# The second feed-forward matmul of a hybrid decoder block as seven block products, with weight sums made by DMA

## What is computed

```python
D_MODEL = 1024; SEQ = 512; D_FF = 4 * D_MODEL
...
        h = rms_norm(x, g_ffn_norm[l])
        x = x + jnp.square(jax.nn.relu(h @ w_ff1[l])) @ w_ff2[l]
```

## Time and profile before

| | |
|---|---|
| median of 3 runs | 634.78 us (633.72 to 634.92) |
| profiled execution, its own time | 633.49 us |
| its span, first to last instruction | 631.8 us |
| granted TensorE clock, mean | 1.000 of full speed |
| PE busy | 617.6 us, 98% of the span |
| DVE, ACT, POOL busy | 325.5, 264.6, 11.0 us |
| HBM read, written | 57.60 MB, 2.10 MB |
| chain that ended last | PE 91%, DVE 4%, ACT 2% |

### The profile page before, as it was taken

The page is one execution under the profiler, slowest core; times in us unless marked ns, Lnnn a source line. Parts: engine busy times, 40 slices in busy tenths (PEclk is TensorE's granted clock), DMA queues, the critical chain, the costliest instruction groups (busy, mean ns, idle before and its releaser), DMA issues.

```text
span 631.8 us, 8695 instructions
## 1 busy us (share of the span) xinstructions
PE 617.6 (98%) x3130; PEld 515.5 (82%) x3130; DVE 325.5 (52%) x577; ACT 264.6 (42%) x503; POOL 11.0 (2%) x31
## 2 busy tenths in 40 slices
PE   7999999999999999999999999999999999999997
PEld 5888677788898888988888888888888888888885
DVE  5699981686688686564333333334433333333323
ACT  7656552737466656462222222223333333222220
POOL 1400000000000000000000000000000000000000
PEclk9999999999999999999999999999999999999999
DMA  8512447342121020004223322332222323322003
GB/s 341 181 42 66 134 137 262 102 167 67 34 68 67 0 68 1 1 1 139 95 99 100 100 100 100 100 98 94 87 89 100 100 100 100 100 100 97 36 0 134
DMA packets 17228, 60.08 MB, mean 95 GB/s; under 512 B 2144, under 2 KB 2432, under 8 KB 17200
## 3 DMA queue, kind: packets, MB, share of 16 engines
q1 hardware_dynamic: 16416, 57.88, 27.0%
q0 software_dynamic: 640, 1.82, 0.9%
q10 hardware_dynamic: 144, 0.01, 0.0%
HBM read 57.60 MB, written 2.10 MB: 94 GB/s over the span
## 4 chain that ended last, share of the span: by engine, by line
PE 91%; DVE 4%; ACT 2%; issue 1%; POOL 0%; DVEq 0%; ACTq 0%; POOLq 0%
PE ps L317 26%; PE ps L319 25%; PE ps L318 25%; PE ps L1687 4%; PE ps L1675 2%; PE ps L1636 1%; PE ps L1422 1%; PE ps L1545 1%; PE ps L1637 1%; DVE ht_lo L955 1%; PE ps L1508 1%; PE ps L1617 1%; DVE w_lo_sb L933 1%; ACT ht_hi L564 1%; PE ps L1597 1%
## 5 line engine op out<-in xcount | busy, mean ns | idle before, releaser
L317 PE MATMUL ps<-ht_hi,w_hi_sb 128*128 128x512 f32 (+1 forms) x280 | 107.7, 385 | 0.0
L319 PE MATMUL ps<-ht_hi,w_lo_sb 128*128 128x512 f32 (+1 forms) x280 | 107.3, 383 | 0.0
L318 PE MATMUL ps<-ht_lo,w_hi_sb 128*128 128x512 f32 (+1 forms) x280 | 107.3, 383 | 0.0
L317 PE MATMUL ps<-w_hi_sb,a_hi 128*128 128x512 f32 x256 | 99.6, 389 | 0.0
L318 PE MATMUL ps<-w_lo_sb,a_hi 128*128 128x512 f32 x256 | 99.6, 389 | 0.0
L319 PE MATMUL ps<-w_hi_sb,a_lo 128*128 128x512 f32 x256 | 99.6, 389 | 0.0
L317 PE MATMUL ps<-w_hi_sb,ht_hi 128*128 128x512 f32 x192 | 82.1, 427 | 3.0 <-DVE ht_lo L955 1.6
L1293 DVE TENSOR_TENSOR w_lo_sb<-raw,w_hi_sb 128x1024 fp32r<-128x1024 f32 x64 | 78.3, 1225 | 10.2 <-ACT w_hi_sb L809 5.0
L319 PE MATMUL ps<-w_hi_sb,ht_lo 128*128 128x512 f32 x192 | 75.3, 392 | 0.0
L318 PE MATMUL ps<-w_lo_sb,ht_hi 128*128 128x512 f32 x192 | 75.1, 391 | 0.0
L1358 DVE TENSOR_TENSOR act_sb<-act_sb (+1 forms) x32 | 22.2, 692 | 102.8 <-ACT act_sb L891 102.8
(11 more groups left out here) (189 smaller groups left out, 791.0 us busy)
## 6 DMA issues: line engine op xcount, KB each, us to landing
raw<-in_w_ff SPq DMA_DIRECT2D x64, 512.0 KB, 3.4
raw<-in_w SPq DMA_DIRECT2D x24, 512.0 KB, 4.6
xs<-in_x SPq DMA_DIRECT2D x8, 512.0 KB, 6.7
raw<-in_cmp_w SPq DMA_DIRECT2D x8, 512.0 KB, 4.7
out_y<-xs SPq DMA_DIRECT2D x3, 512.0 KB, 2.7
raw<-in_w_c SPq DMA_DIRECT2D x4, 304.0 KB, 2.8
spw_sb<-in_sp_w POOLq DMA_DIRECT2D x1, 512.0 KB, 3.6
grow_ffn<-in_g_ffn POOLq DMA_DIRECT2D x1, 512.0 KB, 3.8
```

Of the source, the lines that this page charges most:

```text
L317: pe.matmul(out, l_hi, r_hi, start=start, stop=False)
L318: pe.matmul(out, l_hi, r_lo, start=False, stop=False)
L319: return pe.matmul(out, l_lo, r_hi, start=False, stop=stop)
```

## The change

A is cut in two row halves (256 rows) and two halves of the hidden units (16 of 32 each), W in two halves of hidden units and two of columns. Eight block products would make the result; the change makes it from seven (Winograd's form of Strassen's scheme). A step J takes one hidden unit of the first half together with its partner of the second half. Six quarters of A per step lie in `aq[:, J]`: A11, A12, A21, A22 and the sums S1 = A21 - A22, S2 = S1 - A11, S3 = A11 - A21, S4 = A12 + S2, with signs as coded, S3 in the place of A21 and S4 in that of S2. The table `PRODUCTS` names for each product the quarter of A, the weight unit, its half and the first PSUM bank. P1, P5, P6, P4 run over 16 steps first (`G1`), then P3, P2, P7 over another 16 (`G2`). Between them ACT and DVE take P1, P6, P5 and P4 out of PSUM into `part`, and `base` adds them to x during four later steps; P3, P2 and P7 are added at the end (`result`).

The sums of W are made in device memory, in a new tensor `forms` (16 steps x 5 x 128 x 512): POOL copies quarters of `w_ff2` and adds to them with `accum_op`, seven DMAs per step, two steps at a time, each DMA behind the one before it of its own step. POOL starts this after `grow_ffn`. SP waits for a step's seven DMAs before it loads its forms. The order of w_ff1's and w_ff2's tiles in device memory changes to match, and some SBUF areas change place.

```diff
+HF = NF // 2
+TH = SEQ // 2
+U0 = NW + NF
+A11, S1, A22, S2, A12, A21 = range(6)
+S4, S3 = S2, A21
+FIRST = slice(A11, S2 + 1)
+SECOND = slice(S4, S3 + 1)
+PRODUCTS = {"P1": (A11, 0, 0, 0), "P5": (S1, 0, 1, 2), "P6": (S2, 1, 0, 4), "P4": (A22, 1, 1, 6),
+            "P3": (S4, 0, 0, 2), "P2": (A12, 0, 1, 0), "P7": (S3, 1, 0, 4)}
+G1, G1_LAST = ["P1", "P5", "P6", "P4"], ["P1", "P6", "P5", "P4"]
+G2, G2_FIRST = ["P3", "P2", "P7"], ["P2", "P3", "P7"]
+LAST_TWO = [("P7", 0, 0), ("P7", 1, 0), ("P3", 0, 0), ("P3", 1, 0), ("P7", 0, 1), ("P7", 1, 1), ("P2", 0, 0),
+            ("P3", 0, 1), ("P3", 1, 1), ("P2", 1, 0), ("P2", 0, 1), ("P2", 1, 1)]
+ENDED = [(p, i) for p, i, e in LAST_TWO if e]
...
+        aq = at("aq", [P, HF, 6, TH], F32, o_a)
+        a_hi = [at("a_hi0", [P, 4, TH], F32R, o_wh + SPARE * UW * 4), at("a_hi1", [P, 4, TH], F32R, o_ht[0])]
+        a_lo = [at("a_lo0", [P, 4, TH], F32R, o_wh + (SPARE + 1) * UW * 4), at("a_lo1", [P, 4, TH], F32R, o_ht[0] + 4096)]
+        nr2 = at("nr2", [P, 2], F32, o_ht[1] + 12288)
+        part = at("part", [P, 2, 3, 512], F32, o_ht[1])
...
+            def first_group(j, i):
+                J = i * 2 + j
+                for unit in range(2):
+                    sp.wait_ge(w_lo, J * 2 + (NS + NF - RAW + 1 + unit))
+                    sp.dma_start(raw[:, 2 * j + unit, :].rearrange("p (h n) -> p h n", h=2),
+                                 forms[J, 2 * unit:2 * unit + 2].rearrange("h p n -> p h n")
+                                 ).then_inc(raw_in[2 * j + unit], 16)
+            def second_group(j, i):
+                k, J = i * 2 + j, i * 2 + (HF + j)
+                sp.wait_ge(w_lo, J * 2 + (NS + NF - RAW + 1))
+                sp.dma_start(raw[:, 2 * j, :].rearrange("p (h n) -> p h n", h=2),
+                             w_ff2[k, 2:4].rearrange("h p n -> p h n")).then_inc(raw_in[2 * j], 16)
+                sp.wait_ge(w_lo, J * 2 + (NS + NF - RAW + 2))
+                sp.dma_start(raw[:, 2 * j + 1, 0:512], forms[k, 4]).then_inc(raw_in[2 * j + 1], 16)
+            for i in range(HF // 2):
+                for j in range(2):
+                    sp.wait_ge(form_made[j], 16 * 7 * (i + 1))
+                    first_group(j, i)
+            with sp.Fori(0, HF // 2) as i:
+                for j in range(2):
+                    second_group(j, i)
...
+            def form_step(k, n):
+                out, src, op = [(slice(0, 2), w_ff2[k, 0:2], None), (slice(2, 4), w_ff2[k, 2:4], None),
+                                (1, w_ff2[k, 0], ALU.add), (2, forms[k, 1], ALU.add), (3, forms[k, 2], ALU.add),
+                                (4, w_ff2[k, 1], None), (4, w_ff2[k, 2], ALU.add)][n]
+                how = {} if op is None else {"accum_op": op, "max_dma_last_dim": 8192}
+                pool.dma_start(forms[k, out], src, **how).then_inc(form_made[k % 2], 16)
+            for i in range(HF // 2):
+                for n in range(7):
+                    for j in range(2):
+                        if i or n:
+                            pool.wait_ge(form_made[j], 16 * (7 * i + n))
+                        form_step(2 * i + j, n)
...
+                if j % 2 == 0:
+                    last = act.activation(aq[:, J, A11:A21 + 1:A21 - A11, :],
+                                          ps[:, 4 + j, :].rearrange("p (h n) -> p h n", h=2), ACT.Relu)
+                else:
+                    act.activation(aq[:, J, A12, :], ps[:, 4 + j, 0:TH], ACT.Relu)
+                    last = act.activation(aq[:, J, A22, :], ps[:, 4 + j, TH:], ACT.Relu)
+                last.then_inc(bank_free, 1)
...
+            def a_high(slot, k, pieces, used, sums):
+                act.wait_ge(w_used, used)
+                act.wait_ge(summed, sums)
+                n = pieces.stop - pieces.start
+                act.activation(a_hi[slot][:, 0:n, :], aq[:, k, pieces, :], ACT.Copy).then_inc(ah_done, 1)
+            def first_group(j, i):
+                J = i * 2 + j
+                for unit in range(2):
+                    form_hi(2 * j + unit, J * 2 + (U0 - 3 + unit), i * 16 + (IN1 + 16))
+                a_high(j, J, FIRST, J * 2 + (U0 - 2), J * 3 + 3)
...
+            act.wait_ge(p_whole, 1)
+            act.activation(part[:, :, 0, :], ps[:, 0:2, :], ACT.Copy).then_inc(p1_kept, 1)
...
+            def sums(i, j):
+                J, n = i * 2 + j // 2, i * 6 + 3 * (j // 2)
+                q = [aq[:, J, k, :] for k in range(6)]
+                dve.wait_ge(squared, i * FR + (j + 1))
+                dve.tensor_tensor(q[S1], q[A21], q[A22], ALU.subtract).then_inc(summed, 1)
+                dve.wait_ge(summed, n + 1)
+                dve.tensor_tensor(q[S3], q[A11], q[A21], ALU.subtract).then_inc(summed, 1)
+                dve.tensor_tensor(q[S2], q[S1], q[A11], ALU.subtract).then_inc(summed, 1)
+            def a_low(slot, k, pieces, count):
+                n = pieces.stop - pieces.start
                 dve.wait_ge(ah_done, count)
-                dve.tensor_tensor(a_lo[:, slot, :], act_sb[:, f, :], a_hi[:, slot, :].bitcast(F32),
+                dve.tensor_tensor(a_lo[slot][:, 0:n, :], aq[:, k, pieces, :], a_hi[slot][:, 0:n, :].bitcast(F32),
                                   ALU.subtract).then_inc(al_done, 1)
+            def fourth_sum(k, count):
+                dve.wait_ge(al_done, count)
+                dve.tensor_tensor(aq[:, k, S4, :], aq[:, k, A12, :], aq[:, k, S2, :], ALU.add).then_inc(summed, 1)
...
+            def second_group(j, i):
+                J = i * 2 + (HF + j)
+                form_lo(2 * j, J * 2 + (H0 + 1))
+                form_lo(2 * j + 1, J * 2 + (H0 + 2), 512)
+                a_low(j, i * 2 + j, SECOND, J + 1)
...
+            second_group(0, 0)
+            dve.wait_ge(p1_kept, 1)
+            dve.wait_ge(p_whole, 2)
+            dve.tensor_tensor(part[:, :, 1, :], ps[:, 4:6, :], part[:, :, 0, :], ALU.add).then_inc(kept, 1)
+            dve.wait_ge(kept, 1)
+            dve.wait_ge(w_used, U0 + 2 * HF - 1)
+            dve.tensor_tensor(part[:, :, 2, :], ps[:, 2:4, :], part[:, :, 1, :], ALU.subtract).then_inc(kept, 1)
+            second_group(1, 0)
+            dve.wait_ge(w_used, U0 + 2 * HF)
+            dve.tensor_tensor(part[:, :, 1, :], part[:, :, 1, :], ps[:, 6:8, :], ALU.add).then_inc(kept, 1)
...
+            def base(t):
+                rows = xs[:, t, :].rearrange("p (h n) -> p h n", h=2)
+                dve.wait_ge(r2_step, 2)
+                dve.wait_ge(kept, 3)
+                dve.scalar_tensor_tensor(out=rows, in0=part[:, t % 2, 0:3:2, :] if t < 2
+                                         else part[:, t % 2, 1:3, :], scalar=stat(rstd, "ffn", t), in1=rows,
+                                         op0=ALU.mult, op1=ALU.add).then_inc(based, 1)
+            for t in range(4):
+                second_group(t % 2, 1 + t // 2)
+                base(t)
...
+            for n, (p, i) in enumerate(ENDED):
+                dve.wait_ge(m_done, n + 1)
+                for c in LAST_COLS if n == len(ENDED) - 1 else [slice(0, 512)]:
+                    result(p, i, c)
...
+            def piece(j, product, i, first, last):
+                a, unit, half, bank = PRODUCTS[product]
+                a -= (FIRST if product in G1 else SECOND).start
+                rows, c = slice(i * P, i * P + P), slice(half * 512, half * 512 + 512)
+                return three(pe, ps[:, bank + i, :], a_hi[j][:, a, rows], a_lo[j][:, a, rows],
+                             w_hi_sb[:, FS[2 * j + unit], c], w_lo_sb[:, FS[2 * j + unit], c], first, last)
+            def step(j, J, products, first=False, last=False):
+                units = [PRODUCTS[p][1] for p in products]
+                pe.wait_ge(al_done, J + 1)
+                for n, p in enumerate(products):
+                    unit = units[n]
+                    if unit not in units[:n]:
+                        pe.wait_ge(w_lo, J * 2 + (NS + NF + 1 + unit))
+                    if first and p == "P6":
                         pe.wait_ge(bank_free, NF)
-                    for b in range(2):
-                        mm = piece(j, t, slice(b * 512, b * 512 + 512), first, False)
-                mm.then_inc(w_used, 1)
...
+                    if first and p == "P2":
+                        pe.wait_ge(p1_kept, 1)
+                    if first and p == "P3":
+                        pe.wait_ge(kept, 2)
+                    if first and p == "P7":
+                        pe.wait_ge(kept, 1)
+                    for i in range(2):
+                        mm = piece(j, p, i, first, last)
+                    if unit not in units[n + 1:]:
+                        mm.then_inc(w_used, 1)
+                    elif last and p in ("P1", "P6"):
+                        mm.then_inc(p_whole, 1)
+            step(0, 0, G1, first=True)
+            step(1, 1, G1)
+            with pe.Fori(1, HF // 2 - 1) as i:
+                for j in range(2):
+                    step(j, i * 2 + j, G1)
+            step(0, HF - 2, G1)
```

(47 more changed lines are left out.)

173 lines of the change are left out of this document (92 added, 81 removed).

## The result

The changed kernel takes **618.28 us** (617.25 to 619.17, 4 runs) against 634.66 us for the kernel before in the same session: a ratio of 0.974 (95% interval 0.972 to 0.977). That is 16.4 us faster, 5.1 us above the forecast of 613.2 and inside the range. The profiled execution took 619.14 us, its span 617.4 us, where 611.9 was forecast for the execution.

What follows compares the result with a forecast made beforehand. PE was taken to bound the kernel. Matmuls -21.8, seam stalls +0.5 and tail -0.3 sum to -21.6 us: 633.49 to 611.9 for the profiled execution, plus 1.3 for the median, 613.2 us; range 611.0 to 623.

Steps and rivals of the forecast that it cites:

- What bounds the kernel: Whole kernel: PE busy 98% of the span; a microsecond of second-stage matmuls removed is a microsecond off the end.
- 96 matmuls, -21.8 us: Second feed-forward stage: 672 matmuls instead of 768, each 226.7 ns, so 21.8 us goes.
- Stalls at the seams, +0.5 us: PE stalls entering the second feed-forward stage and between its two product groups: +0.5 us (0 to 2).
- The chain: POOL's serial DMA rounds making weight forms: 34.8 us a pair of steps (28 to 52), 49.3 allowed before PE waits.
- bounds of 3.6 and 9.6: Low and high price in us of a round of two 256 KB adds in POOL's DMAs; 5.2 was taken.
- Traffic, 0 (to 3): Forms' DMA traffic beside attention and first stage: cost 0, up to 3 us if an output projection load comes late.
- The tail, -0.3: From last matmul's start to the end: shorter last DVE instructions against bunched output stores, -0.3 us (-0.8 to +1.0).
- the late forms: Rival, chance 0.14: POOL's forms come too late for the first group, PE waits; 715 us at 12 us per add round.
- the formula: Late forms' cost at the first group's end: PE waits 8p - 394 us, for p us a pair beyond 49.3.
- The lock of POOL's queue: Rival, chance 0.03: DVE holds up POOL's DMA issues, a pair costs 52.3 us, the end 24 us more: 637 us.
- The crowding case: Rival, chance 0.10: transfers crowd out other loads or short steps stall PE, 0.3 us in 32 steps, giving 623 us.
- the forecast case itself: Whole kernel: the forecast as it stands, between 611.3 and 616 us, chance 0.73.

Runs made afterwards that it cites:

- the clean pair of profiles: Kernel before, and changed kernel with 64 bytes' shift of the weight forms' areas plus identity tile at a multiple of 128 bytes: 612.58 us, ratio 0.966.
- the run of copies: Changed kernel with each adding DMA of POOL made a plain copy of the same source, destination and pieces: 618.79 us (one run).

## Why the prediction was right, and where it was off

- **What bounds the kernel**: right. A saved matmul was a saved 226.7 ns; the clean pair of profiles gives -22.5, of which the matmuls are 21.8 and the tail 0.5.
- **96 matmuls, -21.8 us**: right as a term, and the step that failed stands beside it: "The matmuls keep their form (128x128 stationary, 512 moving columns), so 96 x 226.7 ns = 21.8 us goes. Everything on PE ahead of 453 us keeps its matmuls." The number and form of the others were kept, and their spacing was not. The diff showed areas changing place, front and prediction named it as a fact, and I gave it no price. It had one: 2.2 us ahead of the first feed-forward stage, 1.6 in it and 2.7 in the second, 6.5 us between the profiles of the changed kernel and the version with 64 bytes put in. By the medians 5.8 us. Without it the time is 612.5, 0.7 us below the forecast.
- **Stalls at the seams, +0.5 us**: none came; the largest interval between two matmuls of the second stage is 0.24 us. The single times were right within 0.1 us for the sums, and the slacks larger than forecast (1.3 us for 0.9, 1.4 us for 0.7). The 0.7 has a slip in it: one step of each group is 5.44 + 4.08 = 9.5 us, where the prediction has 9.3.
- **The chain**: 36.2 us a pair for 34.8. "As if the 512 KB it reads were copied" was the right choice between the bounds of 3.6 and 9.6: a 256 KB add lands in 4.9 us and a 512 KB copy in 4.8. The Trainium skill (Collectives: The Full Stack, Part 3) has an adding DMA at about half the rate of a copy, and the runs go that way: 4.9 us from issue to landing beside 2.9, 1.7 times as long.
- **Traffic, 0 (to 3)**: right, shown by the run without the chain.
- **The tail, -0.3**: -0.6, and -0.5 in the clean pair. The reading behind it was not exact: the kernel before ended on two instructions of 256 columns as well; what is gone is the 512-column one that started behind the last matmul.
- **The rivals**: the late forms did not happen. The run with a late start shows that they would have cost somewhat less than the formula says (with the last landing at 587.5 us against the 523 at which its expectation wants it, 64 us; measured 59.7) and 2.3 us of clock on top. The lock of POOL's queue did not happen: with DVE busy 71% of 120 to 284 us, plain issues took 0.49 to 0.52 us and adds 0.76 to 0.86, and in the run of copies all took 0.49 to 0.51. The rule that I cited from the Trainium skill (SBUF — State Buffer, two separate sides) had no effect here, as the prediction expected of copies that read PSUM; every DVE copy of that stretch reads PSUM, so no run tries the rule where it would apply. The crowding case gave the right side of the range (618.3 lies between 616 and 623) for a wrong reason: it laid the loss on DVE and the loads, and neither delayed PE.

What stays open: why the distance between the operands matters and why its sign does, and why six intervals behind an odd step are still slow. The range of the forecast case itself, 611.3 to 616, did not hold the time.

## What to carry to other kernels

When a change moves SBUF areas, work out for each dense matmul where the moving and the stationary operand start, modulo 256 bytes, and keep the two equal; in this kernel the wrong distance costs 1 to 3% of every 512-column matmul and shows in no list of waits. Other shapes and formats were not tried, apart from the transposes, which lost nothing. Compare spacings from start to start in stages that the change did not touch: they show such a cost at once. Work made by DMA in device memory far ahead of its use is free here, as long as the serial chain, priced by its rounds from issue to landing, ends in time.

## What the runs showed of the hardware that I had not expected

- The spacing of 128x512 matmuls, each with its own weight load, depends on the distance of the operands' starts modulo 256 bytes: 226.7 ns at 0, 228.9 at +64, 232.4 at 128, 233.3 at -64, +32 and -32 (the two values of 32 from one run). All areas moved together change nothing.
- An adding DMA of 256 KB within device memory lands in 4.9 us, a plain copy in 2.9, and 0.76 us instead of 0.49 go to its issue on POOL.
- A DMA share of 0.72 in the first feed-forward stage (the changed kernel with 64 bytes put in) leaves its matmuls 226.7 ns apart, as 0.31 does in the kernel before. From 120 to 284 us the share rose from 0.14 to 0.74, and without the chain the kernel is no faster (617.92 for 618.28 us).
